# Prompt attention with the values as weights, in column halves for two heads at once, and the transposed result turned back per row tile

## The reference, cut to what matters

```python
def _select_attend(q, qi, wi, ki_all, q_pos, gather_kv):
    ...
    _, sel = lax.top_k(score, topk)
    valid = sel <= q_pos[None, :, None]
    k_sel, v_sel = gather_kv(sel)
    logits = jnp.einsum('bqhgd,bqkhd->bqhgk', qg, k_sel) * (HEAD_DIM ** -0.5)
    logits = jnp.where(valid[:, :, None, None, :], logits, -jnp.inf)
    p = jax.nn.softmax(logits, axis=-1)
    o = jnp.einsum('bqhgk,bqkhd->bqhgd', p, v_sel)
```

## Time and profile before

| | us |
|---|---|
| median of 3 runs | 1938.31 (1937.66 to 1951.98) |
| the profiled execution | 1930.21 |
| its span | 1928.4 |
| prompt attention in it, from the first matmul (689.37) to the last multiplication's end (863.24) | 173.87 |
| busy over the span: PE, PEld, DVE, ACT | 1642.7, 790.1, 848.7, 383.6 |

### The profile page before, as it was taken

The page is one execution under the profiler, slowest core; times in us unless marked ns, Lnnn a source line. Parts: engine busy times, 40 slices in busy tenths (PEclk is TensorE's granted clock), DMA queues, the critical chain, the costliest instruction groups (busy, mean ns, idle before and its releaser), DMA issues. The chain is left out here.

```text
span 1928.4 us, 20694 instructions
## 1 busy us (share of the span) xinstructions
PE 1642.7 (85%) x7569; PEld 790.1 (41%) x7570; DVE 848.7 (44%) x1902; ACT 383.6 (20%) x762; POOL 206.2 (11%) x180
## 2 busy tenths in 40 slices
PE   7598999999999979989990859993499999999970
PEld 1354333344443356775440644552233333333320
DVE  0314558999999324543215563335311211111115
ACT  2112343232111135432224341110000000000002
POOL 0000001110000000000001450000011111111112
PEclk9799999999999969999995779996699999999995
DMA  9202121331333240007427025320799999999934
GB/s 323 90 1 78 45 88 61 130 129 65 140 122 119 77 163 1 1 12 297 175 89 260 1 91 195 98 82 14 285 343 361 364 359 351 343 352 329 326 84 185
DMA packets 128865, 319.69 MB, mean 166 GB/s; under 512 B 15422, under 2 KB 22846, under 8 KB 126211
## 3 DMA queue, kind: packets, MB, share of 16 engines
q1 hardware_dynamic: 112572, 235.52, 34.6%
q0 software_dynamic: 16128, 82.85, 12.9%
q10 hardware_dynamic: 72, 0.07, 0.0%
HBM read 279.83 MB, written 38.59 MB: 165 GB/s over the span
## 5 line engine op out<-in xcount | busy, mean ns | idle before, releaser
L2437 PE MATMUL banks<-arena 128*64 x1008 | 439.0, 595 | 5.2 <-issue 2.4
L2438 PE MATMUL banks<-arena 128*64 128x512 f32 x1008 | 439.1, 595 | 0.0
L997 PE MATMUL banks<-arena 128*128 128x512 f32 (+2 forms) x960 | 383.9, 556 | 0.3 <-ACT arena L1139 0.3
L997 PEld LDWEIGHTS banks<-arena 128*128 128x128 f32 (+1 forms) x960 | 167.3, 188 | 219.9 <-issue 214.3
L2437 PEld LDWEIGHTS banks<-arena 128*64 128x64 f32 x1008 | 136.7, 137 | 282.5 <-issue 282.5
L1293 DVE TENSOR_SCALAR_CACHE_REDUCE arena<-arena 128x384 uint8<-128x384 f32 (+3 forms) x224 | 246.0, 1142 | 3.4
L2438 PEld LDWEIGHTS banks<-arena 128*64 128x64 f32 x1008 | 136.7, 137 | 0.0
L2507 DVE TENSOR_TENSOR arena<-arena,banks 128x256 f32<-128x256 f32 x42 | 15.8, 418 | 262.1 <-PE banks L2438 262.1
L2018 PE MATMUL banks<-arena 128*128 128x512 f32 (+1 forms) x288 | 127.6, 602 | 2.9 <-DMA arena<-in_w_out 2.9
L2489 ACT ACTIVATE arena<-banks 128x512 f32<-128x512 f32 x21 | 12.5, 597 | 465.1 <-PE banks L2438 465.1
L1554 DVE CUSTOM_DVE_ANT_0 arena<-banks,arena 128x512 f32<-128x512 f32 (+3 forms) x96 | 51.4, 575 | 81.2 <-PE banks L1490 81.2
(11 more groups left out here) (397 smaller groups left out, 1957.3 us busy)
## 6 DMA issues: line engine op xcount, KB each, us to landing
arena<-in_w SPq DMA_DIRECT2D x63, 2048.0 KB, 12.4
arena<-in_ada_w SPq DMA_DIRECT2D x12, 2048.0 KB, 8.3
arena<-in_w_in SPq DMA_DIRECT2D x7, 2048.0 KB, 7.9
arena<-in_ada_final_w SPq DMA_DIRECT2D x4, 2048.0 KB, 8.1
arena<-in_x_prompt SPq DMA_DIRECT2D x1, 4096.0 KB, 25.2
arena<-in_w_out SPq DMA_DIRECT2D x2, 2048.0 KB
arena<-in_x_prompt SPq DMA_DIRECT2D x8, 512.0 KB, 4.2
tmp_yslot<-arena POOLq DMA_DIRECT2D x8, 512.0 KB, 5.0
```

The lines of the kernel that those rows point to most:

```text
L997: ins = pe.matmul(ps[0:m, ring[n] % 2, 0:cols], lhs(a), rhs(a), start=(a == 0), stop=(a == KD - 1))
L2437: pe.matmul(ps[0:HP, bank, :], x[:, 0:HP], Wt[:, bass.ds(at, 1), off:off + width].rearrange("p o a -> p (o a)"), **kw)
L2438: return pe.matmul(ps[HP:P, bank, :], x[:, HP:P], Wt[:, u, off:off + width], **kw)
```

## The change

The weighing swaps its operands. Before, the turned P (128 keys x 128 queries) was the weights and 64 columns of values moved; the result had queries in partitions. Now 64 columns of values are the weights, one head in the left and one in the right column half of the array, and the 128 columns of P move; the result has head width in partitions (two heads, 128) and queries in columns. So it has to be turned back: VectorE copies the finished bank to a new buffer `oT` (`taken`), TensorE turns its four blocks into bank 5 (`back`), and VectorE multiplies from there by the reciprocal (`out`, now two instructions). `back` and `out` are in the second unit of the next tile (`BACK`, units 5, 9, ... 29), for the last tile at the end.

For the two heads of a pair to be weighed together, a slot now holds the same piece `c` of both heads (`half`), where before it held, from tile 4 on, both pieces of one head.

```diff
+    oT = ar.view(o, 4, P); o += 512
...
+    BACK = {4 * i + 5: i for i in range(NT - 2)}
+    def half(n, q):
+        return divmod(q - 2 * first[n], 2)
+    def copied(q):
+        return q // 2 + (len([n for n in BACK if 2 * first[n] + 1 < q]) if q % 2 else 0)
...
-                x, c = divmod(q - 2 * first[n], pieces(n))
+                c, x = half(n, q)
                 pe.wait_ge(s["e"], 2 * n + x + 1)
                 if q >= 2:
-                    pe.wait_ge(s[("pca", "pcd")[q % 2]], q // 2)
+                    pe.wait_ge(s[("pca", "pcd")[q % 2]], copied(q))
...
             def weigh(n, q):
-                x, c = divmod(q - 2 * first[n], pieces(n))
-                i, h = n // 4, head(n, x)
+                c = half(n, q)[0]
+                i, pp = n // 4, n % 4 // 2
                 if q == 2 * first[4 * i]:
                     pe.wait_ge(s["ev"], i + 1)
                     if i >= 2:
                         pe.wait_ge(s["o"], i - 1)
-                pe.wait_ge(s[("pca", "pcd")[q % 2]], q // 2 + 1)
+                for x in range(2):
+                    pe.wait_ge(s[("pca", "pcd")[x]], copied(q + x) + 1)
                 for v in range(width(n, c) // P):
                     u = 4 * c + v
-                    ins = pe.matmul(ps[:, 6 + i % 2, h * HD:(h + 1) * HD], PT[q % 4][:, v, :], z[:, u, VC + (h // 2) * HD:VC + (h // 2 + 1) * HD],
-                                    start=(u == 0), stop=(u == i))
-                ins.then_inc(s["pv"], 1)
+                    for x in range(2):
+                        ins = pe.matmul(ps[x * HD:(x + 1) * HD, 6 + i % 2, n % 4 * P:(n % 4 + 1) * P], z[:, u, VC + (2 * pp + x) * HD:VC + (2 * pp + x + 1) * HD],
+                                        PT[(q + x) % 4][:, v, :], start=(u == 0), stop=(u == i))
+                        if (v + 1) * P == width(n, c):
+                            ins.then_inc(s["pv"], 1)
+            def back(i, q):
+                pe.wait_ge(s["o"], i + 1)
+                pe.wait_ge(s["pcd"], copied(q) + 1)
+                for u in range(4):
+                    ins = pe.transpose(ps[:, 5, u * P:(u + 1) * P], oT[:, u, :], k.ident)
+                ins.then_inc(s["bk"], 1)
 
...
                         weigh(owner[q - 2], q - 2)
-                        weigh(owner[q - 1], q - 1)
+                    if n in BACK and q == 2 * first[n]:
+                        back(BACK[n], q + 1)
             weigh(NU - 1, q)
-            weigh(NU - 1, q + 1)
+            pe.wait_ge(s["o"], NT - 1)
+            back(NT - 2, q + 1)
...
+            def taken(i):
+                ve.wait_ge(s["pv"], 2 * first[4 * i + 4])
+                if i:
+                    ve.wait_ge(s["bk"], i)
+                ve.tensor_copy(oT.rearrange("p a b -> p (a b)"), ps[:, 6 + i % 2, :]).then_inc(s["o"], 1)
 
             def out(i):
                 n = slice(H * i, H * i + H)
                 ve.wait_ge(s["e"], n.stop)
                 ve.reciprocal(rden[:, n], den[:, n]).then_inc(s["rd"], 1)
                 ve.wait_ge(s["rd"], i + 1)
-                ve.wait_ge(s["pv"], 2 * first[4 * i + 4])
-                ve.tensor_tensor(A[:, i, :].rearrange("p (h d) -> p h d", d=HD), ps[:, 6 + i % 2, :].rearrange("p (h d) -> p h d", d=HD),
-                                 rden[:, n].unsqueeze(2).broadcast_to([P, H, HD]), ALU.mult).then_inc(s["o"], 1)
+                ve.wait_ge(s["bk"], i + 1)
+                for pp in range(2):
+                    heads = slice(4 * pp, 4 * pp + 4)
+                    ins = ve.tensor_tensor(A[:, i, :].rearrange("p (y x g d) -> p y g x d", y=2, x=2, g=2)[:, pp], ps[:, 5, :].rearrange("p (y g x d) -> p y g x d", y=2, g=2, x=2)[:, pp],
+                                           rden[:, n][:, heads].rearrange("p (x g) -> p g x", g=2).unsqueeze(3).broadcast_to([P, 2, 2, HD]), ALU.mult)
+                ins.then_inc(s["pcd"], 1)
...
-                    if n % 4 == 0 and n and q == 2 * first[n]:
-                        out(n // 4 - 1)
+                    if q == 2 * first[n]:
+                        if n % 4 == 0 and n:
+                            taken(n // 4 - 1)
+                        if n in BACK:
+                            out(BACK[n])
+            taken(NT - 2)
             out(NT - 2)
```

More of the change, by code:

```diff
@@ L1437, in prompt_attention @@
     L.append(ar.view(O_KT + 2 * SEQ, 2, SEQ))
+    oT = ar.view(o, 4, P); o += 512
     assert o <= O_K0, o
-    names = "past ks kc tr ev mm l e pt pca pcd pv rd o".split()
+    names = "past ks kc tr ev mm l e pt pca pcd pv rd o bk f".split()
     s = {n: k.sem("at_" + n) for n in names}
@@ L1557, in turned @@
             def turned(n, q):
-                w = width(n, (q - 2 * first[n]) % pieces(n))
+                w = width(n, half(n, q)[0])
                 ve.wait_ge(s["pt"], q + 1)
```

## The result

The changed kernel takes **1953.05 us** (median of 12 runs, 1950.74 to 1960.74) against 1938.18 for the kernel before (median of 12 runs, 1930.83 to 1951.98). The ratio is **1.0075, interval 1.0058 to 1.0093**: slower by 14.9 us where +12.2 was forecast, inside the range and within 1%. The profiled execution took 1950.86 us (span 1949.1), that of before 1930.21 (1928.4).

A forecast was written before the change was run, and what follows sets the result against it. Most slots were taken as bound by the circle through VectorE and PSUM bank 5; 3.2+0.8-0.4+11.2-0.7-0.5-1.4 = +12.2 us on the median of 1938.3 gave 1950 us, range 1935 to 1965.

The forecast's parts named there:

- Bank 5's circle: Attention slots: logits, two minima, VectorE's copy emptying bank 5, next odd turn, next logits; sets the period, 3.76 us in tile 3.
- the first rival: Attention stage: no slot waits for bank 5 and the halved weighing comes through, -23.6 us, 1915 us; chance 0.05.
- Order by piece, +3.2: First slots of tiles 4 to 6: VectorE now copies 512-column pieces instead of short ones, lengthening bank 5's circle; +3.2 us.
- Turning back, 7 x 1.6: Second unit of each later tile: four transposes and two multiplications through bank 5 add 1.6 us, seven times; +11.2 us.
- Tail, -1.4: Last four slots, without logits: weighing gains 3.2 us, turning back behind the last matmul costs 1.75; together -1.4 us.
- Column halves overlap: Weighing: two heads' matmuls run together; the rival that they run one after another gave 1965 us, chance 0.04.
- the multiplications cost what the earlier trace say: Turning back: two multiplications, 0.77 us together; rival of 0.8 us multiplications and a second wait gave 1958 us, chance 0.05.
- The clock: Rival: idling in bank-5 slots drops TensorE to 1.2 GHz, about 1.4 us a slot, up to 1995 us; chance 0.08.
- the forecast's 0.10: Each slot's weighing: going back from column halves to full turns costs about 0.10 us, 5 us over 48 slots.

The follow-up runs named there:

- 3: The kernel before with every second block of the weighing left out: stage 169.3 us against 173.9; its total, 1956.7 us, doesn't compare.
- 1: The kernel before with VectorE's copy out of bank 5 moved ahead of the masked minima: 1932.26 us, ratio 0.9953.
- 2: The changed kernel with VectorE's copy out of bank 5 moved ahead of the masked minima: 1916.37 us, ratio 0.9879.
- 4: The changed kernel without the turning back, its output left transposed: stage 179.4 us, 13.9 less than with it; total 1964.63 us, with more expert matmuls.
- 5: The kernel before with the pieces in the new order and P still as weights: 1961.94 us in one run, stage 197.7 us.
- 6: The changed kernel with filling matmuls into bank 4 ahead of even turns in tiles 2 to 7: 1954.64 us, ratio 1.0082.
- 7: The changed kernel with the bank-5 copy ahead of the minima and the queries of tiles 2 to 4 turned at the unit's end: 1906.43 us, ratio 0.983.
- 10: The same kernel as 7, run again: 1906.02 us, ratio 0.9815 to the kernel before.
- 8: As 7, with late queries from the second tile on and tiles 3 to 6 turned back in the accumulator's own bank: 1908.98 us, ratio 0.9843.

## Why the prediction held, and where it was off

**Bank 5's circle bounds most slots: right, and shown** from three sides: slots of one form kept their length to 0.01 us under the change (3.76, 3.89), kept it with 256 passes left out (3), and lost it when only VectorE's order was changed (1, 2). ScalarE's exponentials are not the bound: in experiment 2 they start 2.00 and 2.72 us behind the logits, before 2.01 and 2.73, and the slot is 0.87 us shorter all the same. The view had put the wait down to ScalarE's exponential in the earlier trace rows; reading the copy as the releaser was the choice on which the whole forecast rested.

The Trainium skill, page "TensorEngine Tiling (Array Packing)", section Performance Considerations, advises to swap operands and tile columns when the moving side has up to 64 columns; by that the first rival would have come true. TensorE's part of it holds here (sixteen passes take 1.03 us and took 1.84). The rival's 1915 comes only with the circle gone: 1916.37 in experiment 2. That agreement in size is partly luck, since the moved copy also shortened slots of before (1) and the clock stayed up (2).

**Order by piece, +3.2: right.** 3.56, 3.67 and 3.78 us are the forecast's periods, with the change, without the turning back (4) and with P as weights (5).

**Turning back, 7 x 1.6: right in kind and size.** +1.63 and +1.64 where the clock was steady; taking it out gives 13.9 us for the whole stage, the clock's share included.

**Tail, -1.4: right**, -1.8 measured. Slots of 2.05 (2.03 forecast), 2.04 for the last weighings, 2.33 behind the last matmul instead of 2.55.

**Column halves overlap, and the multiplications cost what the earlier trace rows say:** those two rivals fell with the first slots read.

**The clock: mis-sized by leaving it out.** The sum held no term for it. I wrote that TensorE "kept the upper level over idle stretches of 1.46 us" and that slots "mostly last as long", and made the fall a rival with a chance of 0.08 and a condition of five slots or more. Four falls came, touching eight slots, five of them by half a microsecond or more: 7.0 us in the profiled execution. My price of 1.4 us a slot lies inside what those five show (0.5 to 2.07). The step that failed is a term put at nothing, on the inference from one idle stretch of a stage that otherwise streams to a stage that idles in nearly every slot. It did not move the result out of the range: forecast +12.2, stage +19.4, medians +14.9. That it did not is partly luck, for between the two profiled executions the loss was 20.7 us, the 1% from which on the rival was to begin. The medians are 14.9 apart and not 20.7 because the profiled execution of before was 8 us under its median and that of after 2 us; why it was, runs without a trace can't tell.

**What stays open** is what sets off a fall. It takes neither the seven long slots (4) nor column halves (5). Filling matmuls left two of four (6). Idle time in every slot would explain the falls in the changed kernel and in 4, and that there are none in 2 and 11, whose slots are dense. It doesn't explain 5, nor experiment 3, which idles as much and never fell after its rise:

```profile
740.00:770.00 30.00, 23.67 (x163) 16.35 (x161) 16.15 (x52) 15.48 (x37) 0.00 (x0) 1.00 0.00 1
```

The changed kernel was busy for 23.03 us of the same 30 and fell at 745. And kernels 7 and 10, which are one and the same, had one fall (at 753 us) and none. So part of it varies between executions of one kernel, and one profile each can't settle a cause.

## What to carry to other kernels

Halving one engine's work is worth only what lies on the circle that closes last: add up the steps from one group to the next along both the engine's own sum and the way through the bank that is free least often, and believe the one that closes to 0.01 us, even where a busy share of 0.99 speaks for the engine. Where a single bank closes it, first put the instruction that frees it ahead of longer work in its in-order queue; here that one line took the changed kernel from +0.75% to -1.2%, a part of it by a clock that stayed up. And where a kernel's later stages depend on its data, compare the stage and count the later stage's instructions before comparing the totals of an experiment that alters the output. Where two stages differ by a few microseconds, first count in each how long the clock was low: of 4.5 us between kernels 7 and 8 that explains 2.9.

## What was not expected of the hardware

The granted clock fell from 2.4 to 1.2 GHz and back inside a stage that never stopped: ahead of the fall at 745 us TensorE was busy for 2.49 of 4.00 us, and it stayed up through 33.41 of 44.00 us later, with 15.51 of 20.00 just before the fall at 772. The busy share of a window alone does not tell the two apart, as experiments 3 and 5 show too. The rise at the stage's start came at 722 us before, near 738 in experiment 1 and near 714 in experiment 2, and the 16 us by which it came later in experiment 1 cost 5.4 us or more, a third of what the whole change is worth; so a single profiled execution compares slots well and stages poorly. In column halves sixteen passes, eight for each of two heads, take 1.03 us, 0.06 each where a pass of before took 0.117, and the change back to the full array lost little enough that the forecast's 0.10 needed no correction.
